# A two-layer transformer kernel on one core: the first normed input tiles made before the last two modulation blocks, their shift added in the rounding and in the remainder

## The chip, the core and the metric

The kernel runs on one core of one Trainium2 chip. A core has a matrix engine (TensorE, in the rows PE, its weight loads PEld), a vector engine (VectorE, DVE), an activation engine (ScalarE, ACT), a general engine (GpSimd, POOL) and a queue that issues transfers (SyncE, SP). Each works through its own list of instructions in order and waits on semaphores for the others. The metric is the time of one execution on the device, in microseconds (us), lower is better.

## What is computed

Two transformer blocks over 512 tokens of width 1024, in float32. The change touches the entry of the first block and its second normalisation:

```python
mod = jax.nn.silu(c) @ w_mod[layer] + b_mod[layer]
mod_c = jax.nn.silu(c_ctx) @ w_mod[layer] + b_mod[layer]
sh1, sc1, g1, sh2, sc2, g2 = jnp.split(mod[:, None, :], N_MOD, axis=-1)
...
h = modulate(rmsnorm(x, norm1_g[layer]), sh1, sc1)       # h * (1 + scale) + shift
hc = modulate(rmsnorm(ctx, norm1_g[layer]), sh1c, sc1c)
...
h2 = modulate(rmsnorm(x, norm2_g[layer]), sh2, sc2)      # and then the gated feed-forward part
```

`x` has 512 tokens, `ctx` 256. Everything behind `h` and `hc` (ten projections, neighbourhood attention, gated linear attention, the feed-forward part, the whole second block) follows from them.

## The kernel before

Activations lie transposed: a tile is 128 features by 512 tokens (a "page", one of 70), so `h` is eight tiles H0 to H7 and `hc` eight tiles HC0 to HC7 of 256 columns. Matrix products run in a split form: every operand is a rounded part (`hi`) and a remainder (`lo`), and each product is three matmuls, hi·hi, hi·lo and lo·hi (lines 1394, 1395, 1396). Weights come in 429 blocks of 128x1024 (`wst`). For a block ACT makes `whi` by a rounding copy (L1624) and POOL makes `wlo` by a subtraction (L2387); this pair is the step `w_split`. There are three raw buffers and four split ones, and the load of block b+3 waits for both halves of block b.

A planner written in Python (`planned`) lists all steps in one order, and each engine then emits its own part of each step in that order. So the place of a step in the list fixes who stands behind whom on each engine.

The entry of the first block runs like this. The modulation vectors come from `w_mod` in blocks of eight pages each: blocks 0 and 1 are the first and second half of the shift, blocks 2 and 3 those of the scale. The step `mod_rows(c)` is eight float32 matmuls with two rows of output (L1409) and a copy by ACT (L1648). The step `mod_columns` turns that row into columns on PE (L1418, 128x2) and adds the bias on DVE (L1893, into `modc`); for the scale DVE also makes A1 = (1 + scale)·gain (L1898). The statistics are squares on ACT (L1630), their sum over tiles on DVE (L1875), a product with a matrix of ones on PE (L1426), then `rstd_act` (L1639 logarithm, L1641 exponential, L1643 copy, with two table loads) and `rstd_dve` (L1881, L1884, L1886).

The step `h_in(k)` makes H(k) and HC(k). DVE multiplies by A1 and the reciprocal root (L1906, L1913) and adds the shift in place (L1909, L1916); ACT rounds (L1654, L1657); POOL subtracts (L2394, L2397). Tiles 0 to 3 use the first halves of shift and scale, tiles 4 to 7 the second. The first main product, called wide here, runs over k = 0 to 7 and for each k over two weight columns (`w_lr`, `wk_g`) and both H(k) and HC(k). Its four PSUM banks are those which the four `mod_columns` used before, so the fourth is free only when DVE has read the last of them (L1893).

Later, at 636 us, the second normalisation does the same with `h2_hi` (DVE L2119 scales, L2122 adds the shift; ACT L1764 rounds) and `h2_lo` (DVE L2128 subtracts), tile by tile between the steps of the first feed-forward product, and some position tables of the second block (L2165 to L2183 on DVE, L1787 to L1791 on ACT) are computed directly after it, ahead of the activation L1769 that frees banks for PE.

Of the kernel before, what the change touches and what calls it, by code (L numbers as in the profile page):

```python
# [10 lines left out]
ACT = mybir.ActivationFunctionType  # L11
# [306 lines left out]
def planned():  # L318
# [25 lines left out]
    for k in range(8, 16):  # L344
        mod_load(k)
    for k in range(24, 32):
        mod_load(k)
    step("load_fixed", "wal")
    step("load_fixed", "tabG")
    for b in range(1, NR):  # L350
        p.w_load(b)
# [5 lines left out]
    for k in range(8):  # L357
        sqc.add(("XC", k // 2), 256 * (k % 2), ("XC", k // 2))
# [16 lines left out]

    mod_rows(0)
    sqx.product("ones", sbk)
    mod_rows(2)
    mod_columns(0, 0)
    sqc.product("ones", sbk)  # L380
    rx = sqx.rstd(1024, "ones", sbk, True)
    mod_rows(1)
    mod_columns(0, 1)
    rc = sqc.rstd(1024, "ones", sbk, True)
    mod_rows(3)
    mod_columns(1, 0)
    for b in range(3):
        p.w_split(b)
    H, HC = [("H", k) for k in range(8)], [("HC", k) for k in range(8)]
    for k in range(8):  # L390
        if k == 4:
            mod_columns(1, 1)
# [5 lines left out]
        pages.give(("hct", k), ("HC", k, "hi"), ("HC", k, "lo"))  # L398
    pages.give(rx, ("hs", 7))
# [784 lines left out]
def program(nc, a, out, p):  # L1184
    with ExitStack() as ctx:
# [189 lines left out]
        def tensor(e):  # L1375
# [35 lines left out]

            def mod_columns(c, half_, part):
# [178 lines left out]
            def ret_values(l, h, i):  # L1591
# [9 lines left out]
                mm, mod_mm, mod_columns, square_sum, to_tokens, mod_sum, gla_gate, gla_state0, gla_states, gla_scores,  # L1601
# [6 lines left out]
        def scalar(e):  # L1608
# [42 lines left out]
            def h_in(k):  # L1651
                clear(("H", k, "hi"))
                w.wait_ge(*when("ht", k))
                e.activation(R(("H", k, "hi")), F(("ht", k)), ACT.Copy).then_inc(*acp.up(("H", k, "hi")))  # L1654
                clear(("HC", k))
                w.wait_ge(*when("hct", k))
                e.activation(R(("HC", k))[:, 0:256], F(("hct", k))[:, 0:256], ACT.Copy).then_inc(  # L1657
                    *acp.up(("HC", k, "hi")))
# [102 lines left out]
            def h2_hi(k):  # L1761
                clear(("H2", k, "hi"))
                w.wait_ge(*when("h2t", k))
                e.activation(R(("H2", k, "hi")), F(("h2t", k)), ACT.Copy).then_inc(*acp.up(("H2", k, "hi")))  # L1764
# [89 lines left out]
        def vector(e):  # L1854
# [46 lines left out]
            def h_in(k):  # L1901
                t, tc = F(("ht", k)), F(("hct", k))[:, 0:256]
# [3 lines left out]
                e.scalar_tensor_tensor(t, F(("X", k)), A1[:, k, 0:1], F(("r", "x")), ALU.mult, ALU.mult).then_inc(  # L1906
# [715 lines left out]
```

## Time and profile before

| | us |
|---|---|
| median of 3 runs | 3139.64 |
| lowest and highest of them | 3133.87, 3141.9 |
| the profiled execution | 3134.09 |
| its span, first to last instruction | 3132.3 |
| PE busy in the span | 2949.9 |
| DVE, ACT, POOL busy in the span | 1435.3, 1202.0, 1234.1 |

The span is that of the profiled execution; the rest of that execution's time, 1.8 us, lies around it. PE's busy time overlaps with its weight loads. The granted clock of TensorE is its mean over a stretch as a share of 2.4 GHz: 0.50 is 1.2 GHz, 1.00 is 2.4 GHz, and over the whole span it was 0.969.

### The profile page before, as it was taken

Reading aid. Unit: us, or ns where it says so; the run is one execution under the profiler, and the core shown is the slowest. Engines: PE = TensorE matmul, PEld = TensorE weight load, DVE = VectorE, ACT = ScalarE, POOL = GpSimd, SP = SyncE. Lnnn points to the kernel's source line nnn. Section 1 sums busy time; section 2 is a strip of 40 time slices with the busy share of each in tenths; the row PEclk is TensorE's granted clock in tenths of the full one; section 3 lists DMA queues with packets and bytes.
Section 4 is the critical chain, followed back from the end, with each engine's and each line's share of the span. In section 5 each row is a group of like instructions: output and inputs, shape, how many; then the busy total and the mean of one; then the engine's idle time right before and its main releaser. Section 6 shows DMA issues by size and latency. Waiting matters only on the chain.

```text
span 3132.3 us, 33658 instructions
## 1 busy us (share of the span) xinstructions
PE 2949.9 (94%) x13120; PEld 2296.9 (73%) x13120; DVE 1435.3 (46%) x1895; ACT 1202.0 (38%) x1737; POOL 1234.1 (39%) x571
## 2 busy tenths in 40 slices
PE   6998999989999898999998999989899999999997
PEld 2787777768888666678686888866666777778886
DVE  5667542451112778664524302257877354151123
ACT  3337653242223545342434322254533333342222
POOL 3213222334445344354343444434533444344442
PEclk8999999989999999999999999989999999999999
DMA  5233221322222210122131222221011222322221
GB/s 208 101 122 123 74 73 68 114 103 94 101 95 108 100 61 21 54 74 96 66 123 66 108 96 99 95 101 68 34 48 61 87 75 87 114 81 94 101 95 61
DMA packets 89342, 278.08 MB, mean 89 GB/s; under 512 B 10048, under 2 KB 10176, under 8 KB 89184
## 3 DMA queue, kind: packets, MB, share of 16 engines
q1 hardware_dynamic: 89184, 275.92, 24.3%
q8 instruction: 105, 1.72, 0.2%
q14 instruction: 53, 0.43, 0.0%
HBM read 268.54 MB, written 7.34 MB: 88 GB/s over the span
## 4 chain that ended last, share of the span: by engine, by line
PE 78%; DVE 15%; ACT 4%; issue 2%; DMA 1%; POOL 0%; SPq 0%; ACTq 0%; DVEq 0%; POOLq 0%
PE bank L1394 23%; PE bank L1396 22%; PE bank L1395 22%; PE bank L1597 2%; DVE pageF L2277 2%; PE bank L1439 1%; PE bank L1572 1%; PE bank L1560 1%; DVE pageF L2084 1%; PE bank L1549 1%; DVE pageF L2351 1%; DVE pageF L2355 1%; PE bank L1426 1%; PE bank L1409 1%; DVE pageR L2150 1%
## 5 line engine op out<-in xcount | busy, mean ns | idle before, releaser
L2387 POOL TENSOR_TENSOR wlo<-wraw,whi 128x1024 fp32r<-128x1024 f32 x429 | 1044.5, 2437 | 1624.8 <-ACT whi L1624 1612.8
L1394 PE MATMUL bank<-pageR,whi 128*128 128x512 f32 x3552 | 1451.7, 409 | 88.9 <-ACT pageR L1779 27.4
L1395 PE MATMUL bank<-pageR,whi 128*128 128x512 f32 x3552 | 1386.6, 390 | 0.0
L1396 PE MATMUL bank<-pageR,wlo 128*128 128x512 f32 x3552 | 1385.9, 390 | 0.0
L1394 PEld LDWEIGHTS bank<-pageR,whi 128*128 128x128 f32 x3552 | 677.3, 191 | 278.7 <-issue 126.4
L1395 PEld LDWEIGHTS bank<-pageR,whi 128*128 128x128 f32 x3552 | 678.5, 191 | 150.2 <-issue 23.6
L1396 PEld LDWEIGHTS bank<-pageR,wlo 128*128 128x128 f32 x3552 | 676.8, 191 | 141.3
L1624 ACT ACTIVATE whi<-wraw 128x1024 fp32r<-128x1024 f32 x429 | 450.5, 1052 | 403.1 <-PE bank L1396 400.0
L1663 ACT ACTIVATE pageR<-pageF 128x512 fp32r<-128x512 f32 x136 | 85.9, 632 | 427.1 <-DVE pageF L2144 207.9
L2277 DVE SCALAR_TENSOR_TENSOR pageF<-pageF,prm 128x497 f32<-128x497 f32 (+9 forms) x180 | 205.3, 1141 | 1.8
L1742 ACT ACTIVATE pageF<-bank,smal 128x512 f32<-128x512 f32 x96 | 66.0, 687 | 202.0 <-DVE smal L2058 201.7
L2139 DVE TENSOR_TENSOR pageF<-bank,pageF 128x512 f32<-128x512 f32 x44 | 30.4, 690 | 209.2 <-PE bank L1396 209.0
L1439 PEld LDWEIGHTS bank<-cst,pageF 128*128 128x128 f32 x564 | 69.4, 145 | 72.8 <-ACT pageF L1742 34.7
L1439 PE MATMUL bank<-cst,pageF 128*128 128x128 f32 x564 | 88.0, 283 | 36.7 <-ACT pageF L1742 22.9
L1875 DVE TENSOR_TENSOR pageF<-pageF 128x512 f32<-128x512 f32 (+1 forms) x60 | 43.6, 726 | 159.0 <-ACT pageF L1630 157.3
L2142 DVE TENSOR_TENSOR pageF<-pageF,bank 128x512 f32<-128x512 f32 x44 | 30.3, 688 | 182.4 <-PE bank L1396 177.4
L1693 ACT ACTIVATE pageF<-bank 128x512 f32<-128x512 f32 (+1 forms) x148 | 82.6, 575 | 80.0 <-PE bank L1439 79.4
L2426 POOL TENSOR_TENSOR pageF<-pageF 128x497 f32<-128x497 f32 (+14 forms) x60 | 79.2, 1320 | 79.8 <-ACT pageF L1826 78.6
L2406 POOL TENSOR_TENSOR pageR<-pageF,pageR 128x512 fp32r<-128x512 f32 x46 | 67.4, 1478 | 107.3 <-ACT pageR L1663 106.8
L2100 DVE SCALAR_TENSOR_TENSOR pageF<-pageF,bank 128x512 f32<-128x512 f32 x64 | 43.9, 685 | 126.8 <-PE bank L1396 126.6
L1923 DVE TENSOR_TENSOR pageR<-pageF,pageR 128x512 fp32r<-128x512 f32 x90 | 65.2, 724 | 64.8 <-ACT pageR L1663 64.8
L2133 DVE TENSOR_TENSOR pageF<-pageF,bank 128x512 f32<-128x512 f32 x22 | 15.1, 688 | 168.0 <-PE bank L1396 163.5
(200 smaller groups left out, 2386.1 us busy)
## 6 DMA issues: line engine op xcount, KB each, us to landing
wraw<-in_wst SPq DMA_DIRECT2D x429, 512.0 KB, 3.4
pageF<-in_wmod SPq DMA_DIRECT2D x96, 256.0 KB, 4.9
pageF<-in_xT SPq DMA_DIRECT2D x16, 256.0 KB, 5.3
pageF<-in_bias SPq DMA_DIRECT2D x16, 256.0 KB, 3.8
kept<-pageF SPq DMA_DIRECT2D x16, 256.0 KB, 4.7
pageF<-kept SPq DMA_DIRECT2D x16, 256.0 KB, 4.2
pageF<-tables SPq DMA_DIRECT2D x8, 256.0 KB, 4.7
out_x<-pageF SPq DMA_DIRECT2D x8, 256.0 KB, 2.0
```

What stands on the lines that cost most here:

```text
L1394: e.matmul(o, hi, xh, start=first, stop=False)
L1395: e.matmul(o, hi, xl, start=False, stop=False)
L1396: i = e.matmul(o, lo, xh, start=False, stop=last)
L1439: t = e.transpose(o[:, 128 * j:128 * j + 128], x[:, c:c + 128], ident)
L1624: e.activation(whi[:, b % NH, :, :], wraw[:, b % NR, :, :], ACT.Copy).then_inc(*whid.up(("whi", b)))
L1663: e.activation(R((*x, "hi")), F(src), ACT.Copy).then_inc(*acp.up((*x, "hi")))
L1693: e.activation(F(dst)[:, 0:n], bank(("tb", dst))[:, 0:n], ACT.Copy).then_inc(*acp.up(dst))
L1742: e.activation(F(("pr", kind, job)), bank(("sc", kind, job)), ACT.Exp, bias=nm, accum_out=sm).then_inc(*fun.up(("pr", kind, job)))
L2277: e.scalar_tensor_tensor(acc, x, c, acc, ALU.mult, ALU.add).then_inc(*vec.up(("tapd", l, m, n)))
L2387: e.tensor_tensor(wlo[:, b % NH, :, :], wraw[:, b % NR, :, :], bc(whi[:, b % NH, :, :]), ALU.subtract).then_inc(*wlod.up(("wlo", b)))
L2406: e.tensor_tensor(R((*x, "lo")), F(src), bc(R((*x, "hi"))), ALU.subtract).then_inc(*low.up((*x, "lo")))
L2426: e.tensor_tensor(acc, acc, F(("tap", l, n))[:, 0:hi - lo], ALU.add).then_inc(*low.up(("tapd", l, m, n)))
```

## The change

Five things are changed.

1. The order of transfers: the pages of `x` are loaded first, then shift and scale blocks 0 and 2, the context, weight block 0, then blocks 1 and 3 with weight blocks 1 and 2 behind them.
2. The order of steps: statistics of `x` go ahead of the squares of `ctx`; four `h_in` stand ahead of `mod_rows(1)` and `mod_rows(3)`; the three `w_split` are spread.
3. A step `warm_up`: six float32 matmuls of 128x512 on constants, in front of the first modulation product.
4. In `h_in` ACT adds the shift as a bias while it rounds, and the remainder is one DVE instruction (value plus shift, minus rounded). The two additions on DVE and the two subtractions on POOL are gone.
5. The same for `h2_hi` and `h2_lo`, where the remainder was on DVE already.

```diff
     for k in range(8):
-        mod_load(k)
-    for k in range(8):
         pages.take(("X", k))
         step("load_x", k)
-    for k in range(8):
-        mod_load(16 + k)
+    for c in (0, 2):
+        for k in range(8):
+            mod_load(8 * c + k)
...
+    sbk.take(("warm",))
+    step("warm_up")
+    sbk.give(("warm",), ("warm",))
     mod_rows(0)
     sqx.product("ones", sbk)
+    rx = sqx.rstd(1024, "ones", sbk, True)
+    for k in range(8):
+        sqc.add(("XC", k // 2), 256 * (k % 2), ("XC", k // 2))
     mod_rows(2)
     mod_columns(0, 0)
+    mod_columns(0, 1)
     sqc.product("ones", sbk)
...
+    p.w_split(0)
...
+    for k in range(4):
+        h_in(k)
+    mod_rows(1)
+    p.w_split(1)
+    mod_rows(3)
+    mod_columns(1, 0)
+    mod_columns(1, 1)
+    for k in range(4, 8):
+        h_in(k)
+    p.w_split(2)
...
+            def warm_up():
+                w.wait_ge(*when("cst"))
+                for i in range(6):
+                    t = e.matmul(bank(("warm",)), ident, cst[:, 0:4, :], start=True, stop=True)
+                t.then_inc(*dot.up(("warm",)))
...
-                w.wait_ge(*when("ht", k))
-                e.activation(R(("H", k, "hi")), F(("ht", k)), ACT.Copy).then_inc(*acp.up(("H", k, "hi")))
+                w.wait_ge(*when("hs", k))
+                e.activation(R(("H", k, "hi")), F(("ht", k)), ACT.Identity, bias=modc[:, k, 0:1]).then_inc(
+                    *acp.up(("H", k, "hi")))
...
-                after()
-                e.tensor_scalar(t, t, modc[:, k, 0:1], None, ALU.add).then_inc(*vec.up(("ht", k)))
...
+                w.wait_ge(*when("H", k, "hi"))
+                e.scalar_tensor_tensor(R(lo), F(("ht", k)), modc[:, k, 0:1], bc(R(("H", k, "hi"))), ALU.add,
+                                       ALU.subtract).then_inc(*vec.up(lo))
...
-                e.tensor_scalar(t, t, modr[:, 8 + k:9 + k], None, ALU.add).then_inc(*vec.up(("h2t", k)))
...
-                e.tensor_tensor(R(lo), F(("h2t", k)), bc(R(hi)), ALU.subtract).then_inc(*vec.up(lo))
+                e.scalar_tensor_tensor(R(lo), F(("h2t", k)), modr[:, 8 + k:9 + k], bc(R(hi)), ALU.add,
+                                       ALU.subtract).then_inc(*vec.up(lo))
```

PE, from its first instruction to the first product with H0, before. L1409 is a modulation product (x8 is one block), L1426 a sum of squares, L1418 the turning into columns.

```order
L1409 MATMUL bank<-pageF,csil 2x512 x8
L1426 MATMUL bank<-pageF,cst 128x512
L1409 MATMUL bank<-pageF,csil 2x512 x8
L1418 MATMUL bank<-cst,pageF 128x2 x4
L1426 MATMUL bank<-pageF,cst 128x256
L1409 MATMUL bank<-pageF,csil 2x512 x8
L1418 MATMUL bank<-cst,pageF 128x2 x4
L1409 MATMUL bank<-pageF,csil 2x512 x8
L1418 MATMUL bank<-cst,pageF 128x2 x8
L1394 MATMUL bank<-pageR,whi 128x512
```

The same stretch of the changed kernel, where lines 1415, 1438, 1430 and 1400 are those of the same four operations and 1421 is the new one.

```order
L1421 MATMUL bank<-cst 128x512 x6
L1415 MATMUL bank<-pageF,csil 2x512 x8
L1438 MATMUL bank<-pageF,cst 128x512
L1415 MATMUL bank<-pageF,csil 2x512 x8
L1430 MATMUL bank<-cst,pageF 128x2 x8
L1438 MATMUL bank<-pageF,cst 128x256
L1415 MATMUL bank<-pageF,csil 2x512 x16
L1430 MATMUL bank<-cst,pageF 128x2 x8
L1400 MATMUL bank<-pageR,whi 128x512
```

All four modulation products still stand ahead of the first main product; the second block's columns moved ahead of the products of the third and fourth.

ACT around the first rounded tiles, before: the last row copies (L1648), the weight roundings (L1624), then the tiles (L1654, L1657).

```order
L1643 ACTIVATE pageF<-bank,prm 128x256
L1648 ACTIVATE pageF<-bank 2x512
L1624 ACTIVATE whi<-wraw 128x1024 x3
L1654 ACTIVATE pageR<-pageF 128x512
L1657 ACTIVATE pageR<-pageF 128x256
```

And now, from the fourth tile (L1666, L1670) to the fifth, with the row copy at line 1660 and the weight rounding at 1636.

```order
L1666 ACTIVATE pageR<-pageF,modc 128x512
L1670 ACTIVATE pageR<-pageF,modc 128x256
L1660 ACTIVATE pageF<-bank 2x512
L1636 ACTIVATE whi<-wraw 128x1024
L1660 ACTIVATE pageF<-bank 2x512
L1666 ACTIVATE pageR<-pageF,modc 128x512
```

The last row copy, which PE's last turning and so the first main product wait for, now stands behind four tiles and two weight roundings.

DVE for one tile, before (first two rows H, then HC):

```order
L1906 SCALAR_TENSOR_TENSOR pageF<-pageF,A 128x512
L1909 TENSOR_SCALAR pageF<-pageF,modc 128x512
L1913 SCALAR_TENSOR_TENSOR pageF<-pageF,A 128x256
L1916 TENSOR_SCALAR pageF<-pageF,modc 128x256
L1906 SCALAR_TENSOR_TENSOR pageF<-pageF,A 128x512
```

And now:

```order
L1919 SCALAR_TENSOR_TENSOR pageF<-pageF,A 128x512
L1924 SCALAR_TENSOR_TENSOR pageF<-pageF,A 128x256
L1929 SCALAR_TENSOR_TENSOR pageR<-pageF,modc,pageR 128x512
L1934 SCALAR_TENSOR_TENSOR pageR<-pageF,modc,pageR 128x256
L1919 SCALAR_TENSOR_TENSOR pageF<-pageF,A 128x512
```

DVE still has four instructions a tile; two of them now wait for ACT's rounding, and POOL's two are gone.

## Rows read from the trace of the kernel before

**Rows 1.** The page, part 1: span, and each engine's busy time.

```profile
span 3132.3 us, 33658 instructions
PE 2949.9 (94%) x13120; PEld 2296.9 (73%) x13120; DVE 1435.3 (46%) x1895; ACT 1202.0 (38%) x1737; POOL 1234.1 (39%) x571
```

**Rows 2.** The chain that ended last, first 60 us: start us, us, what.

```profile
20.98 8.70 PE bank L1409 x16
...
30.66 6.96 PE bank L1409 x16
...
37.95 6.96 PE bank L1409 x16
...
47.06 2.33 DVE pageF L1916
49.39 2.76 DVE pageF L1906
```

**Rows 3.** The timeline, PE: start us, us, engine, line, what [idle before <-releaser].

```profile
55.88 0.77 PE L1394 MATMUL bank<-pageR,whi 128*128 128x512 f32 x1 [9.89 <-POOL pageR L2394]
...
64.50 0.58 PE L1394 MATMUL bank<-pageR,whi 128*128 128x256 f32 x1 [5.08 <-DVE modc L1893]
```

**Rows 4.** The first transfer of constants (timeline, then time to landing) and the squares of x.

```profile
1.65 0.42 SPq L1301 DMA_DIRECT2D cst<-in_cst  x1
...
cst<-in_cst SPq DMA_DIRECT2D x1, 320.0 KB, 3.1
...
12.65 4.68 ACT L1630 ACTIVATE pageF<-pageF 128x512 f32<-128x512 f32 x7 [0.34 <-DMA pageF<-in_xT]
```

**Rows 5.** The timeline, ACT and DVE, context squares, statistics and a row copy.

```profile
22.82 2.73 ACT L1630 ACTIVATE pageF<-pageF 128x256 f32<-128x256 f32 x8 [5.48 <-DMA pageF<-in_cT]
23.57 3.60 DVE L1875 TENSOR_TENSOR pageF<-pageF 128x256 f32<-128x256 f32 x7 [4.78 <-ACT pageF L1630]
...
30.33 1.28 ACT L1639 ACT_TABLE_LOAD   x1
...
34.16 0.67 ACT L1643 ACTIVATE pageF<-bank,prm 128x512 f32<-128x512 f32 x1
...
42.70 0.42 DVE L1886 SCALAR_TENSOR_TENSOR pageF<-pageF 128x256 f32<-128x256 f32 x1
...
44.94 0.59 ACT L1648 ACTIVATE pageF<-bank 2x512 f32<-2x512 f32 x1 [2.83 <-PE bank L1409]
```

**Rows 6.** Busy time by window: stretch, length, PE, PEld, DVE, ACT, POOL, PEclk, DMA share, GB/s.

```profile
64.40:68.80 4.40, 4.30 (x14) 3.72 (x15) 4.16 (x8) 1.47 (x3) 2.74 (x2) 0.50 0.02 6
68.80:75.00 6.20, 6.20 (x37) 5.41 (x37) 6.06 (x9) 2.11 (x4) 4.10 (x5) 1.00 0.00 0
...
667.40:672.90 5.50, 5.46 (x13) 4.38 (x14) 4.07 (x6) 2.69 (x4) 1.12 (x1) 0.50 0.00 0
```

**Rows 7.** The timeline, DVE and POOL, as the wide product ends.

```profile
79.77 7.03 POOL L2387 TENSOR_TENSOR wlo<-wraw,whi 128x1024 fp32r<-128x1024 f32 x3 [0.21 <-ACT whi L1624]
...
81.52 0.69 DVE L1931 TENSOR_TENSOR pageF<-bank,tabG 128x512 f32<-128x512 f32 x1 [3.29 <-PE bank L1396]
...
85.12 2.23 DVE L1938 TENSOR_TENSOR pageF<-pageF 128x512 f32<-128x512 f32 x1
```

**Rows 8.** Second normalisation, 635 to 668 us: single lines (durations ns min/median/max) and timeline.

```profile
L2119 DVE SCALAR_TENSOR_TENSOR pageF<-pageF,A x8: 742/746/2884, 635.8 to 649.8; 128x512 f32<-128x512 f32 x8
...
L2122 DVE TENSOR_SCALAR pageF<-pageF,modr x8: 485/486/488, 636.6 to 652.7; 128x512 f32<-128x512 f32 x8
...
638.15 0.68 DVE L2128 TENSOR_TENSOR pageR<-pageF,pageR 128x512 fp32r<-128x512 f32 x1
...
657.21 1.06 ACT L1624 ACTIVATE whi<-wraw 128x1024 fp32r<-128x1024 f32 x1 [2.38 <-PE bank L1396]
...
663.35 0.63 ACT L1787 ACTIVATE pageF<-pageF 128x512 f32<-128x512 f32 x1 [3.77 <-DVE pageF L2181]
...
666.70 0.60 ACT L1769 ACTIVATE pageF<-bank 128x512 f32<-128x512 f32 x1
...
667.44 0.77 PE L1394 MATMUL bank<-pageR,whi 128*128 128x512 f32 x1 [4.89 <-ACT pageF L1769]
```

More of the change, by code:

```diff
@@ L343, in planned @@
     p.w_load(0)
[L344 to L347, printed above, removed]
+    for c in (1, 3):
+        for k in range(8):
+            mod_load(8 * c + k)
+        p.w_load(1 + c // 2)
     step("load_fixed", "wal")
     step("load_fixed", "tabG")
-    for b in range(1, NR):
-        p.w_load(b)
     step("silu_c")
@@ L356, in planned @@
         sqx.add(("X", k), 0, ("X", k))
-    for k in range(8):
-        sqc.add(("XC", k // 2), 256 * (k % 2), ("XC", k // 2))
     def mod_rows(c):
@@ L1600, in tensor @@
             mine = {f.__name__: f for f in (
-                mm, mod_mm, mod_columns, square_sum, to_tokens, mod_sum, gla_gate, gla_state0, gla_states, gla_scores,
+                mm, mod_mm, warm_up, mod_columns, square_sum, to_tokens, mod_sum, gla_gate, gla_state0, gla_states, gla_scores,
                 gla_out, na_scores, na_values, mla_scores, mla_values, conv_mean, ret_scores, ret_values)}
@@ L1652, in h_in @@
                 clear(("H", k, "hi"))
-                w.wait_ge(*when("ht", k))
-                e.activation(R(("H", k, "hi")), F(("ht", k)), ACT.Copy).then_inc(*acp.up(("H", k, "hi")))
+                w.wait_ge(*when("hs", k))
+                e.activation(R(("H", k, "hi")), F(("ht", k)), ACT.Identity, bias=modc[:, k, 0:1]).then_inc(
+                    *acp.up(("H", k, "hi")))
                 clear(("HC", k))
-                w.wait_ge(*when("hct", k))
-                e.activation(R(("HC", k))[:, 0:256], F(("hct", k))[:, 0:256], ACT.Copy).then_inc(
-                    *acp.up(("HC", k, "hi")))
+                w.wait_ge(*when("hcs", k))
+                e.activation(R(("HC", k))[:, 0:256], F(("hct", k))[:, 0:256], ACT.Identity,
+                             bias=modc[:, k, 1:2]).then_inc(*acp.up(("HC", k, "hi")))
             def halves(x, src, made, lane):
@@ L1762, in h2_hi @@
                 clear(("H2", k, "hi"))
-                w.wait_ge(*when("h2t", k))
-                e.activation(R(("H2", k, "hi")), F(("h2t", k)), ACT.Copy).then_inc(*acp.up(("H2", k, "hi")))
+                w.wait_ge(*when("h2s", k))
+                e.activation(R(("H2", k, "hi")), F(("h2t", k)), ACT.Identity, bias=modr[:, 8 + k:9 + k]).then_inc(
+                    *acp.up(("H2", k, "hi")))
             def ffn_act(s, og, ou, r):
@@ L2120, in h2_hi @@
                     *vec.up(("h2s", k)))
-                after()
-                e.tensor_scalar(t, t, modr[:, 8 + k:9 + k], None, ALU.add).then_inc(*vec.up(("h2t", k)))
             def h2_lo(k):
@@ L2427, in tap @@
                     *low.up(("tapd", l, m, n)))
-            mine = {f.__name__: f for f in (w_split, h_in, halves, in_sum, tap)}
+            mine = {f.__name__: f for f in (w_split, halves, in_sum, tap)}
             for kind, *what in p.steps:
```

35 lines of the change are left out of this document (11 added, 24 removed).

## The prediction

> **What bounds the kernel now.** The page's first part comes first: PE is busy for 2949.9 of 3132.3 us [rows 1], so only about 180 us of the span are open to an edit that leaves PE's work alone, and this one does. I looked for them in the chain of waits and then in PE's timeline. In the first 60 us the chain runs through the four modulation products on PE and then through DVE [rows 2]: the fourth product ends at 37.95 + 6.96 = 44.9 us. From there on DVE instructions that should take 0.35 and 0.75 us take 2.33 and 2.76 us; they lie beside POOL's three weight subtractions. PE starts the wide product only at 55.88 us, released by POOL's remainder of H0, and after 3.3 us of it stands still again until 64.50 us, because DVE has not read the last modulation bank, which is queued behind four tiles [rows 3]. The clock is low there (0.50, 1.2 GHz) until 68.8 us [rows 6]. The second place is near 636 us: the chain is on DVE through the eight tiles and the tables behind them, and PE idles 4.89 us before 667.44 us [rows 8]. Elsewhere the change touches nothing.
>
> **The change, part by part.** I walk the changed order with durations of before, on the axis of the same profile.
>
> Warm-up and block 0. The constants are issued at 1.65 us and land 3.1 us later [rows 4], 4.8 us. A float32 matmul of 512 columns is two records; at the full clock 16 records take 6.96 us, 0.43 each, at the low one twice that [rows 2]. Twelve warm-up records thus cost 5.2 to 10.3 us; I take 8, half of them at each clock, so PE is free at 12.8 us. That costs nothing by itself: the pages of block 0 now come behind those of x, and the sixteenth page was there at about 16.7 us (the start of the last of the squares, 12.65 + 4.68 - 0.63) [rows 4]. Block 0 is then done at 12.8 + 6.9 = 19.7 us, the sum of squares at 20.6, block 2 at 27.5 (29.68 before, 20.98 + 8.70).
>
> Statistics. ACT does those of x first, two tables of 1.28 and three passes of about 0.65 us, [rows 5], 20.3 to 24.9 us. The context squares (2.73) follow to 27.6, the row copy (0.59) to 28.2. DVE does its three for x from 24.3 to 26.4 and then the seven context additions (3.60) [rows 5], to 30.0; these are later than before (27.2) and now set the pace. Then PE's sum 0.7, on ACT 0.47 + 1.28 + 0.42 + 0.46 (its table preloaded), DVE's three of 0.42: the context's reciprocal root is ready at about 34.6 us. It was ready at 42.70 + 0.42 = 43.1 us [rows 5], but the first tile had to wait for block 1 of the shift and DVE began it at 45.4. So the tiles begin 10.8 us earlier.
>
> Four tiles. Per tile DVE now has scale 0.69 and 0.42, a wait of about 0.28 for ACT's rounding (0.64 behind the first), remainder 0.69 and 0.45, 2.6 us with gaps. The remainder as one instruction with the shift doesn't exist before; between L2128's 0.68 and L2119's 0.75 [rows 8] the bounds are close, and I take 0.69. Rounding with a bias is bounded by the same operation from PSUM, 0.67 [rows 5], against 0.63 for the plain copy. The one weight subtraction in this stretch costs DVE one stall, 2.76 - 0.69 = 2.1 us [rows 2]. Four tiles: 34.6 + 2.1 + 10.4 = 47.1 us; ACT's last rounding there ends some 0.7 earlier, 46.4. Behind it on ACT stand the row copy, the weight rounding and the last row copy, 0.59 + 1.04 + 0.59 [rows 5, 8], 48.7 us, then 0.4 for the turning. PE's products of blocks 1 and 3 run from 30.6 to 44.6, or to 48.0 if the clock falls in the gap before them: hidden either way. **The wide product begins at 49.2 us**, and nothing in it waits: DVE frees the last bank at once, since it idles for just that column, and tiles 4 to 7 come every 2.6 us from 50 on, while PE needs the fifth at about 60.
>
> The wide product. Before, 3.3 us of it ran at the low clock before the stop, and 81.5 - 64.5 = 17.0 us behind it, 4.4 of these at the low clock [rows 3, 6, 7]. In one piece with 4.4 us at the low clock it lasts 20.3 - (3.3 / 2) = 18.7 us. It ends at 67.9, against 81.5: **13.6 us earlier**. Bounds: without the DVE stall and with a short low stretch 16; with two stalls and 3 us more on ACT's queue 10. Behind it DVE and PE alternate in the chain; all loads and weight steps hang on steps that moved too, so I let the whole shift pass. One stall of 1.5 us (L1938, 2.23 instead of 0.69, beside POOL's backlog [rows 7]) may go; POOL's fifth subtraction would end within 0.1 us of it, so I take 0 and keep 1.5 for the range.
>
> Of the shared path between DVE and POOL, the rows show that a DVE instruction with two SBUF tiles waits for a running POOL subtraction [rows 2] and that one fed from PSUM, L1931, does not [rows 7]. The Trainium skill, "SBUF — State Buffer", section "SBUF: two separate sides", says the same as an exclusive lock held for the whole instruction, and so speaks against putting 16 more remainders with two SBUF inputs on DVE. By it, each remainder could also hold off POOL's weight halves for its 0.69 us; the sum would be about 0.3 us worse.
>
> Second normalisation. Eight additions of 0.486 us leave DVE [rows 8]; the remainder grows by at most 0.07. The first remainder waits for one addition less of its own tile and one of the next, so PE starts 0.9 us earlier (638.1) and, being the slower from then on, ends this product at 661.6. DVE's tables start 3.4 earlier. But the rounding of the fourth weight block on ACT, which stands ahead of the table functions, waits for PE (L1624 at 657.21 [rows 8]), so it moves by 0.9 only: 656.3 + 1.06, table 1.28, first function at 658.6 (663.35 before). From that function to PE's restart it was 667.44 - 663.35 = 4.1 us [rows 8]: 662.7. **PE restarts 4.8 us earlier.** With one more DVE stall in the tables it is 3; if the gap, now 1.1 us, leaves the clock high, half of the 5.5 us at 0.50 [rows 6] come on top, 7.5 at most.
>
> Sum: 13.6 + 4.8 = 18.4 us. The profiled execution took 3134.1, so 3115.7; the median of before lies 5.5 higher, and against it the sum is 3139.6 - 18.4 = **3121.2, say 3121 us**.
>
> **Rivals.**
> The second place gives little: the tables' DVE instructions run into POOL's subtractions as before (L2119's longest was 2.884 us [rows 8]) and fill the gap. Then 13.6 alone, 3126. For it: two stalls of this kind are there now. Against: the additions are in the chain themselves.
>
> The head start is handed back: behind the wide product something pinned ends the gain, for instance modulation pages of the later blocks that arrive when they did. If only 3 us of the head survive: 3139.6 - 3 - 4.8 = 3132. For it: DVE holds much of the chain up to 200 us and the early transfers as a whole are no smaller. Against: the queue's order there is unchanged and each load waits for a page or a weight half that is earlier.
>
> Slower: TensorE's clock doesn't rise in the head. Then the warm-up and every modulation record costs 0.43 us more. Ahead of the wide product are 64 such records and the wide product's own start; at the low clock throughout they would add 64 x 0.43 = 27.5 us against a gain of 18.4, so 3149. It turns into a loss once 43 of the 64 records are slow. Against: in every busy stretch of before the clock rose within a few us (at 68.8 after work from 64.5 [rows 6]). The Trainium skill, "TensorE: Matmul & The Clock Gate", section "What's actually happening", has the low clock as the default after idling; by it the warm-up is lost again if PE then waits, as it will between 44.6 and 49.2, and I have priced the wide product's start as low for that reason.
>
> **How the numbers follow.** Main case 0.62 (3114 to 3127), only the head 0.17 (3126), handed back 0.13 (3132), low clock 0.04 (3149), and 0.04 for no difference at all. The range takes the largest gain, 16 + 1.5 + 7.5 = 25, with the runs' own spread (the lowest of before lies 5.8 under its median) down to 3109, and the smallest, 10 + 3 = 13, plus 4 for the median's own uncertainty, up to 3131. A difference of 0.3%, 9.4 us, is about the least that can be told from none here: the line is at 3130.2. Faster: 0.62 + 0.17 and a third of the handed-back case, 0.83. Slower by as much: 0.04. Within: 0.13.
>
> **What would show it.** In the changed profile: block 2's product ends near 27.5; the first DVE scale at 34.6, the first L1400 at 49.2 with no second stop; the low clock ends by 54; the rope multiplication (L1931 before) starts at 67.9; each later landmark up to 600 us stands 13 to 14 us earlier. At the second place the idle time before PE's restart is 1 us, not 4.9. I am wrong if the first L1400 is past 53, if the shift at 300 us is under 10, or if DVE's remainders take over 1 us on average.

## The result and the profile after

The changed kernel takes 3116.2 us in the median of 4 runs (3112.3 to 3118.1); the kernel before, beside it, 3136.8 (3133.2 to 3141.9). The ratio is 0.9932, 95% interval 0.9912 to 0.9951. The forecast was 3121, in a range of 3109 to 3131.

The page's first part answers to [rows 1]:

```profile
span 3115.6 us, 33638 instructions
PE 2952.5 (95%) x13132; PEld 2298.8 (74%) x13132; DVE 1419.1 (46%) x1887; ACT 1203.0 (39%) x1737; POOL 1217.3 (39%) x555
```

The span is 16.7 us shorter, PE's work the same but for 12 warm-up records; DVE lost 16 us and POOL 17. How much of either was in the way is a matter of places. PE in the head, to set beside [rows 2, 3] (timeline: start us, us, engine, line, what, count, [idle before <-releaser]):

```profile
6.37 8.45 PE L1421 MATMUL bank<-cst 128*128 128x512 f32 x12 [6.37 <-DMA cst<-in_cst]
14.76 7.03 PE L1415 MATMUL bank<-pageF,csil 128*2 128x512 f32 x16
21.72 1.12 PE L1438 MATMUL bank<-pageF,cst 128*128 128x512 f32 x2
22.77 7.03 PE L1415 MATMUL bank<-pageF,csil 128*2 128x512 f32 x16
...
32.78 15.59 PE L1415 MATMUL bank<-pageF,csil 128*2 128x512 f32 x32
48.70 0.41 PE L1430 MATMUL bank<-cst,pageF 2*128 2x2 f32 x4 [0.33 <-ACT pageF L1660]
50.13 0.40 PE L1430 MATMUL bank<-cst,pageF 2*128 2x2 f32 x4 [1.02 <-ACT pageF L1660]
50.46 0.50 PE L1400 MATMUL bank<-pageR,whi 128*128 128x512 f32 x1
```

PE's 9.89 us of waiting ahead of the first main product and the stop of 5.08 us inside it are gone; blocks 1 and 3 now run beside the tiles. DVE, ACT and POOL in that stretch:

```profile
36.38 0.74 DVE L1919 SCALAR_TENSOR_TENSOR pageF<-pageF,A 128x512 f32<-128x512 f32 x1
37.05 2.57 DVE L1924 SCALAR_TENSOR_TENSOR pageF<-pageF,A 128x256 f32<-128x256 f32 x1
...
42.25 0.75 DVE L1929 SCALAR_TENSOR_TENSOR pageR<-pageF,modc,pageR 128x512 fp32r<-128x512 f32 x1 [0.39 <-ACT pageR L1666]
...
45.03 0.75 DVE L1929 SCALAR_TENSOR_TENSOR pageR<-pageF,modc,pageR 128x512 fp32r<-128x512 f32 x1 [0.40 <-ACT pageR L1666]
...
67.27 0.69 DVE L1950 TENSOR_TENSOR pageF<-bank,tabG 128x512 f32<-128x512 f32 x1 [3.97 <-PE bank L1402]
67.99 2.84 DVE L1954 TENSOR_TENSOR pageF<-bank,tabG 32x512 f32<-32x512 f32 x4
70.87 2.72 DVE L1957 TENSOR_TENSOR pageF<-pageF 128x512 f32<-128x512 f32 x1
...
44.28 0.72 ACT L1666 ACTIVATE pageR<-pageF,modc 128x512 fp32r<-128x512 f32 x1 [1.66 <-DVE pageF L1919]
...
48.56 1.04 ACT L1636 ACTIVATE whi<-wraw 128x1024 fp32r<-128x1024 f32 x1
49.50 0.57 ACT L1660 ACTIVATE pageF<-bank 2x512 f32<-2x512 f32 x1
...
36.55 2.79 POOL L2405 TENSOR_TENSOR wlo<-wraw,whi 128x1024 fp32r<-128x1024 f32 x1 [36.11 <-ACT whi L1636]
49.74 2.38 POOL L2405 TENSOR_TENSOR wlo<-wraw,whi 128x1024 fp32r<-128x1024 f32 x1 [10.40 <-ACT whi L1636]
63.48 9.56 POOL L2405 TENSOR_TENSOR wlo<-wraw,whi 128x1024 fp32r<-128x1024 f32 x4 [11.36 <-ACT whi L1636]
```

One remainder starts 2.78 us after the other (45.03 - 42.25), which is the time of a tile. The rope multiplication (L1950, DVE's first step on the wide product's result) stands at 67.27, [rows 7] had it at 81.52: 14.3 us gained.

Second normalisation, PE's two starts, the fourth weight block's rounding and first table function on ACT, and DVE's table steps:

```profile
628.68 0.77 PE L1400 MATMUL bank<-pageR,whi 128*128 128x512 f32 x1 [7.51 <-DVE pageR L2145]
...
654.24 0.47 PE L1400 MATMUL bank<-pageR,whi 128*128 128x512 f32 x1 [1.14 <-ACT pageF L1783]
...
647.76 1.06 ACT L1636 ACTIVATE whi<-wraw 128x1024 fp32r<-128x1024 f32 x1 [4.38 <-PE bank L1402]
...
650.14 0.63 ACT L1801 ACTIVATE pageF<-pageF 128x512 f32<-128x512 f32 x1
...
643.86 2.51 DVE L2194 TENSOR_SCALAR pageF<-pageF 128x512 f32<-128x512 f32 x1
...
648.58 0.43 DVE L2199 TENSOR_SCALAR pageF<-pageF 128x512 f32<-128x512 f32 x1
```

The restart moved from 667.44 [rows 8] to 654.24, 13.2 us, 3.8 of them won here (the shift just ahead was 9.4), and the low clock that followed it in [rows 6] is absent, which gives 2.5 more.

POOL lost time here, too. Its first weight subtraction in this stretch lasts 5.70 us, and 2.86 in the kernel before:

```profile
632.39 5.70 POOL L2405 TENSOR_TENSOR wlo<-wraw,whi 128x1024 fp32r<-128x1024 f32 x1 [14.33 <-ACT whi L1636]
...
635.08 0.74 DVE L2138 SCALAR_TENSOR_TENSOR pageF<-pageF,A 128x512 f32<-128x512 f32 x1
```

and before:

```profile
643.58 2.86 POOL L2387 TENSOR_TENSOR wlo<-wraw,whi 128x1024 fp32r<-128x1024 f32 x1 [15.98 <-ACT whi L1624]
```

In the changed kernel DVE ran scalings and remainders without a gap until 635.82 us, and 2.3 us later POOL was done. The timeline shows no wait of PE's between 628.68 and 654.24 us, so PE lost nothing by it.

To see where the shift grows and shrinks, I paired PE's matmuls of two traces one by one, counted from the end (fillers left out), and took the difference of their starts. Times are on the axis of before. "Changed" is the profiled run above; "again" and "beside" are two more of the same kernel; the experiments of the other rows follow below. The last column is the whole shift.

| us | 70 | 100 | 140 | 300 | 320 | 600 | 660 | 690 | end |
|---|---|---|---|---|---|---|---|---|---|
| changed | -14.3 | -15.9 | -13.6 | -14.9 | -10.4 | -9.5 | -9.4 | -15.8 | -16.7 |
| again | -13.6 | -15.2 | -15.3 | -12.6 | -11.9 | -11.4 | -11.6 | -17.9 | -19.1 |
| beside | -12.8 | -14.4 | -14.7 | -13.7 | -13.7 | -13.6 | -14.1 | -17.2 | -18.4 |
| head only | -15.4 | -17.0 | -15.0 | -16.4 | -16.4 | -16.4 | -16.5 | -16.4 | -17.9 |
| second place only | -0.3 | -0.3 | 0.2 | 5.5 | 5.9 | 6.2 | 6.0 | 2.8 | 1.7 |
| order only | -9.1 | -10.8 | -10.5 | -10.6 | -10.6 | -10.6 | -10.6 | -10.5 | -11.9 |
| instructions only | -0.7 | -2.3 | 1.8 | 0.3 | 0.3 | 0.3 | -0.1 | -3.3 | -4.6 |
| no warm-up | -12.9 | -14.5 | -10.1 | -11.4 | -6.8 | -5.9 | -5.8 | -12.1 | -12.9 |
| rows first | -15.5 | -17.1 | -12.4 | -13.9 | -13.9 | -13.8 | -14.3 | -17.4 | -18.6 |
| fillers | -15.0 | -16.6 | -14.8 | -16.9 | -16.8 | -16.8 | -19.1 | -20.2 | -21.4 |
| tables late | -16.6 | -18.2 | -18.3 | -18.3 | -18.3 | -18.3 | -18.6 | -26.0 | -26.4 |
| tables late, fillers | -15.8 | -17.4 | -16.8 | -14.3 | -13.6 | -13.1 | -15.5 | -22.8 | -23.1 |

The 1.6 us that every row but "second place only" gains from 70 to 100 us come between 84 and 90 us. The kernel before is at the low clock there (85.9 to 89.3 us), as is "second place only", and the others are not at that work.

### The profile page after: what moved, and what is told of

Same layout as the page of the kernel before. It is cut to its first block, busy times and chain, and to the rows that moved or that the text cites. A ratio compares the mean times of both kernels' runs of the same rounds, so it can differ in the third digit from the quotient of the medians.

```text
span 3115.6 us, 33638 instructions
## 1 busy us (share of the span) xinstructions
PE 2952.5 (95%) x13132; PEld 2298.8 (74%) x13132; DVE 1419.1 (46%) x1887; ACT 1203.0 (39%) x1737; POOL 1217.3 (39%) x555
## 4 chain that ended last, share of the span: by engine, by line
PE 78%; DVE 15%; ACT 4%; issue 2%; DMA 1%; POOL 1%; SPq 0%; DVEq 0%; ACTq 0%; POOLq 0%
PE bank L1400 23%; PE bank L1402 22%; PE bank L1401 22%; PE bank L1609 2%; DVE pageF L2295 2%; PE bank L1451 1%; PE bank L1584 1%; PE bank L1572 1%; PE bank L1561 1%; DVE pageF L2103 1%; DVE pageF L2373 1%; DVE pageF L2369 1%; DMA pageF<-in_wmod 1%; DVE pageR L2168 1%; PE bank L1600 1%
## 5 line engine op out<-in xcount | busy, mean ns | idle before, releaser
L1676 ACT ACTIVATE pageR<-pageF 128x512 fp32r<-128x512 f32 x136 | 85.9, 632 | 425.0 <-DVE pageF L2162 208.1
L2160 DVE TENSOR_TENSOR pageF<-pageF,bank 128x512 f32<-128x512 f32 x44 | 30.2, 687 | 182.4 <-PE bank L1402 177.4
L1889 DVE TENSOR_TENSOR pageF<-pageF 128x512 f32<-128x512 f32 (+1 forms) x60 | 43.0, 717 | 149.6 <-ACT pageF L1642 148.0
L1895 DVE TENSOR_TENSOR pageF<-pageF 128x512 f32<-128x512 f32 (+1 forms) x41 | 26.9, 656 | 141.5 <-ACT pageF L1653 141.5
```

What stands on the lines that cost most here:

```text
L1676: e.activation(R((*x, "hi")), F(src), ACT.Copy).then_inc(*acp.up((*x, "hi")))
```

## The experiments

My theory was that of the prediction: the head and the second place are two separate gains, the head's being that the tiles no longer wait for blocks 1 and 3 and that POOL's remainders and DVE's additions are out of the way. The rivals were that one of the two gives nothing, that it is all order (or all instructions), and that the clock decides.

### Each place alone

Head only: the second normalisation keeps its old instructions.

```diff
-                e.scalar_tensor_tensor(R(lo), F(("h2t", k)), modr[:, 8 + k:9 + k], bc(R(hi)), ALU.add,
-                                       ALU.subtract).then_inc(*vec.up(lo))
+                e.tensor_tensor(R(lo), F(("h2t", k)), bc(R(hi)), ALU.subtract).then_inc(*vec.up(lo))
...
+                e.tensor_scalar(t, t, modr[:, 8 + k:9 + k], None, ALU.add).then_inc(*vec.up(("h2t", k)))
```

> The changed kernel with its second normalisation put back (DVE adds the shift, ACT copies, plain subtraction). Theory A (the two places add up, as the shift between the two traces says: 14.3 us at the end of the wide product, 4 us more at PE's restart near 667 us and some 2 us of clock behind it): 4 to 6 us slower than the changed kernel, so 14 to 17 us faster than before, ratio 0.995. Its PE idle time before the restart is again 4 to 5 us. Rival B (the tables' DVE work would have been hidden anyway): within 1.5 us of the changed kernel.

Measured 3118.4 us (3116.1 to 3124.0), ratio 0.9954, interval 0.9941 to 0.9966: 16.9 us under the median of before beside it, as expected, but only 2 us over the changed kernel's median, where 4 to 6 were expected. PE's wait before its restart is 4.94 us, and its shift does not move between 600 and 690 us. Second place only: the kernel before with the opposite of this diff and nothing else.

> The kernel before with only the second normalisation changed. Theory A: 4 to 6 us faster than before, ratio 0.9985; nothing differs ahead of 636 us, PE's idle time before the restart falls from 4.9 to about 1 us. Rival B: no difference.

Measured 3133.2 us (3127.0 to 3138.1), ratio 0.9992, interval 0.9983 to 1.0002: for itself not to be told from nothing. Its trace shows a gain all the same, 3.4 us between 600 and 690 us in the table. That is under the 4 to 6 expected, and PE's wait before its restart fell to 2.72 us and not to 1. The 5.5 us it lost before 300 us lie where no instruction differs from the kernel before, nearly all of them in one low-clock stretch of 10.2 us at 218.7 us. The kernel before has no such stretch there, and in this trace no wait of PE's stands right ahead of it.

So both places give. In the traces of the table the whole head is worth 12.8 to 16.6 us at 70 us, and the second place, with the tables where they were, 3.4 to 6.5.

### Order and instructions, apart

Order only: the changed order of loads and steps with the warm-up, but the old instructions at both places (shift added by DVE, remainder of H on POOL).

```diff
-                w.wait_ge(*when("hs", k))
-                e.activation(R(("H", k, "hi")), F(("ht", k)), ACT.Identity, bias=modc[:, k, 0:1]).then_inc(
-                    *acp.up(("H", k, "hi")))
+                w.wait_ge(*when("ht", k))
+                e.activation(R(("H", k, "hi")), F(("ht", k)), ACT.Copy).then_inc(*acp.up(("H", k, "hi")))
```

> The new order of transfers and steps and the warm-up, but all normed tiles by the old instructions (shift by a DVE addition, remainders of the first tiles on POOL). Theory A (the order is most of the gain, the instructions set the pace of a tile): a tile takes DVE 3.4 us, as tiles 4 to 7 did before, against 2.6, so four tiles cost 3.2 us more and the wide product starts at about 53.7 us instead of 50.5 and ends at 71; with the old second normalisation the whole is 10 to 11 us faster than before. Rival C (the fused instructions are most of the gain, since DVE and POOL block each other): under 5 us faster than before.

Measured 3126.1 us (3122.2 to 3130.8), ratio 0.9975, interval 0.9966 to 0.9985. Its DVE and PE:

```profile
46.87 1.37 DVE L1921 TENSOR_SCALAR pageF<-pageF,modc 128x512 f32<-128x512 f32 x1
...
51.44 0.58 PE L1430 MATMUL bank<-cst,pageF 2*128 2x2 f32 x4 [4.44 <-ACT pageF L1660]
...
53.37 0.80 PE L1400 MATMUL bank<-pageR,whi 128*128 128x512 f32 x1
```

In the second and the fourth tile DVE's additions, beside POOL's remainders, take 1.3 to 1.4 us; one at 55.68 us, with POOL at rest, took 0.49. The first four tiles last from 35.50 to 50.45 us, 15.0, where the changed kernel has 12.8 (36.38 to 49.14). PE waits 4.44 us, starts the main product 2.9 us later than the changed kernel, and is at the low clock for 6.8 us from 51.4 on. So the start was 53.4 us for the 53.7 expected.

Instructions only: the kernel before with the new instructions at both places, old order, no warm-up (the edit is the reverse of the one above, in the kernel before).

> The new instructions in both places, but the old order of transfers and steps and no warm-up. Theory A: the first main matmul waits for POOL's first weight half (49.2 us), PE stops again until DVE has done four tiles with three stalls, 45.4 + 4 x 2.6 + 3 x 2.1 = 62 us (64.5 before), so some 2.5 us at the head and 5 at the second place: 6 to 9 us faster than before. Rival C: over 12 us faster than before.

Measured 3131.0 us (3127.6 to 3135.6), ratio 0.9992, interval 0.9983 to 1.0001: 4 us, less than I expected, and within the interval nothing. PE and DVE:

```profile
52.25 0.77 PE L1394 MATMUL bank<-pageR,whi 128*128 128x512 f32 x1 [5.99 <-DVE pageR L1923]
...
63.05 0.58 PE L1394 MATMUL bank<-pageR,whi 128*128 128x256 f32 x1 [6.04 <-DVE modc L1901]
...
49.29 2.81 DVE L1923 SCALAR_TENSOR_TENSOR pageR<-pageF,modc,pageR 128x512 fp32r<-128x512 f32 x1 [2.52 <-ACT pageR L1660]
```

The main product starts 3.6 us earlier than in [rows 3], not at the 49.2 us expected, and then stands still for 6.0 us instead of 5.1: the last bank still waits behind four tiles. At 70 us order alone has 9.1 us, instructions alone 0.7, both together 14.3 (13.6 and 12.8 in the other two traces). The sum of the parts is 9.8, so 3.0 to 4.5 us are in neither alone.

It is not that PE waits for something else in the old order: it waits for these tiles there too. But the first tile gives back what is saved. DVE's first remainder now needs ACT's rounding, which stands behind three weight roundings, and DVE idles 2.52 us for it. Then two weight subtractions hold DVE up (2.81 us for the remainder shown, 2.46 for the next). The four tiles take 17.2 us instead of 18.9. And the low clock lasts until 69 us in both kernels, so that of 1.45 us of shift at 68 us 0.7 are left at 70. The new order spreads the three weight roundings, and a tile then costs 2.8 us.

The order of transfers and the order of steps were only ever changed together; what each gives alone is open.

### The warm-up

```diff
-    sbk.take(("warm",))
-    step("warm_up")
-    sbk.give(("warm",), ("warm",))
```

> The changed kernel without its six warm-up matmuls. Theory A (the warm-up is neutral: without it the first modulation product starts when its first page has landed, near 12 us, at the low clock, and ends near 21.5 us as it does now, at 21.8): within 2 us of the changed kernel. Rival D (the warm-up carries the head: later modulation products stay at the low clock without it): 5 us or more slower than the changed kernel, with the wide product starting at 55 us or later.

Measured 3115.6 us (3115.3 to 3121.2), ratio 0.9933, interval 0.9919 to 0.9946, the same as with it. Its shift at 70 us is -12.9, within the -12.8 to -14.3 of the three traces with it, and its main product starts at 50.27 us; so much for the rival's 55. Its first product starts earlier and takes longer, and ends at 21.64 us, with the warm-up at 21.79:

```profile
13.00 8.64 PE L1412 MATMUL bank<-pageF,csil 128*2 128x512 f32 x16 [13.00 <-DMA pageF<-in_wmod]
```

### The last row copy ahead of the weight rounding

In the changed kernel the copy that PE's last turning waits for stands behind a weight rounding of 1.04 us. This moves it ahead.

```diff
     mod_rows(1)
-    p.w_split(1)
     mod_rows(3)
     mod_columns(1, 0)
     mod_columns(1, 1)
+    p.w_split(1)
```

> The changed kernel with the second weight block's rounding behind the last two row copies and the turning instead of between them. If the wide product waits for ACT's queue, as the chain of the changed kernel says (the last row copy starts at 49.50 us, right behind a rounding of 1.04 us, while PE's product was done at 48.4): it starts 0.9 us earlier and the kernel is 0.5 to 1.5 us faster than the changed one, too little to be told in its time but plain in its trace. If something else ends that wait: the start stays at 50.4 to 50.5 us.

Measured 3113.3 us (3108.9 to 3115.5), ratio 0.9923, interval 0.9911 to 0.9936. The main product starts at 49.24, not 50.46, and 70 us is reached 1.2 us earlier than in the changed kernel. The median is 2.9 us lower, but the intervals overlap.

### The clock at the second place

Eight filler matmuls stand in PE's wait for the second normalisation; nobody reads their product, and nothing is left out.

```diff
         r = sq.rstd(1024, "ones", sbk, warm=True)
+        sbk.take(("warm2",))
+        step("warm_up", "warm2", 8)
+        sbk.give(("warm2",), ("warm2",))
```

> The changed kernel with eight idle float32 matmuls on constants put into PE's wait for the second normalisation (7.5 us idle at 621 to 628.7 us). Its output is not touched. If the low clock behind that wait is due to the idling: the granted clock stays at 1.00 there, PE's product after it runs at full speed from the start, and PE gains 2.5 us, of which up to 1.5 may be handed back where PE then waits for the tables; kernel 1 to 2.5 us faster. If the clock falls whatever PE does there: no gain, low clock until 634 us as now.

Measured 3118.0 us (3112.7 to 3122.3), ratio 0.994, interval 0.9926 to 0.9954: no gain. PE's two starts there:

```profile
621.44 0.47 PE L1403 MATMUL bank<-pageR,whi 128*128 128x512 f32 x1 [0.64 <-DVE pageR L2149]
...
647.05 0.77 PE L1403 MATMUL bank<-pageR,whi 128*128 128x512 f32 x1 [3.57 <-ACT pageF L1787]
```

The clock did stay high, and the shift at 650 us was 2.3 us larger than ahead of the place. But PE then waits 3.57 us for the gate's eviction (L1787, ACT emptying the bank that PE needs) behind the tables' ACT passes, and works at the low clock again. In this trace a clock bought ahead of a join with a slower engine was mostly idle time at the join.

### The same kernel again, twice

> The changed kernel once more, for a second trace. Between 300 and 350 us the changed kernel lost 4.5 us of its lead in the first trace, where PE stood still for 4.7 us in both kernels and the low clock behind it lasted 13.7 us instead of 3.4. If that is a matter of the single execution: another length of the low stretch here, and another lead at 350 us. If it belongs to the change: 13.7 us again.

3115.0 us, its only run. Low-clock stretches have other lengths in it than in the first profile. The clearest case is around 290 us, where PE waits 4.6 to 4.9 us in every trace. Windows of the changed kernel (stretch, length, busy time of PE, PEld, DVE, ACT, POOL, then PEclk, DMA share, GB/s):

```profile
290.00:295.00 5.00, 5.00 (x15) 4.08 (x16) 4.96 (x6) 2.57 (x6) 2.57 (x1) 0.50 0.26 100
295.00:300.00 5.00, 5.00 (x17) 3.94 (x16) 2.06 (x5) 0.32 (x1) 0.19 (x1) 0.50 0.73 241
300.00:305.00 5.00, 5.00 (x24) 4.33 (x23) 1.97 (x4) 0.46 (x2) 0.00 (x0) 0.73 0.21 77
```

and of the run beside the last two kernels below:

```profile
290.00:295.00 5.00, 3.80 (x15) 3.15 (x15) 4.90 (x8) 3.82 (x9) 1.32 (x1) 0.66 0.48 172
295.00:300.00 5.00, 5.00 (x30) 4.21 (x30) 4.42 (x8) 0.78 (x2) 1.43 (x1) 1.00 0.47 155
```

13.7 us of low clock (1.2 GHz) in the first, 3.4 us in the second, with the same instructions. It is this that took the first profile from -14.9 to -10.4 us at 300 to 320 us; it is no cost of the change.

### Tables behind the first gates

The experiment that follows from the two above: if PE's restart waits for the tables' passes on ACT, plan the tables one slot later (and keep the rows first).

```diff
     def side_tables():
+        yield from pause(1)
         pages.take(("posi",))
```

> The changed kernel with two moves: the second weight block's rounding stands behind the last two row copies (as in the run of that one move), and the position tables' plan starts one slot later, so that the first sine table's load and three ACT passes (1.28 + 0.63 + 0.64 + 0.72 us) stand behind the first two gates of the feed-forward's wide group and not ahead of them. Theory: in the traces PE stood 1.1 us (changed kernel) or 2.7 us (the run with the rows first) before its restart for the gate's eviction that waits for those passes, and in the second of these a low clock of 3.4 us followed. With the tables behind, PE's wait there is at most 0.8 us and no low clock follows: 2 us + 1.7 us better than the run with the rows first at 690 us (shift against the kernel before about -21 there, -17.4 in that run), median near 3110 against its 3113.3. Rival: the tables' passes only push the later gates back, the wait turns up again within 20 us, and the time stays at 3113.

> As the run before it, plus eight filler matmuls in PE's wait for the second normalisation, whose product nobody reads (the work the kernel needs is all there). In the earlier run with fillers PE kept the full clock through its restart and was 2.3 us ahead at 650 us, and gave that back because it then waited for the tables' ACT passes and fell to the low clock for 6.8 us. Theory: with the tables out of the way the 2.3 us stay: shift at 690 us about -23, median near 3108. Rival: the time at 690 us is set by ACT and DVE, not by PE's clock, and both runs agree within 1 us.

> The changed kernel itself, unaltered, beside the two above on the same chip: 3116 within its spread of 3112 to 3118. Its low clock behind PE's wait near 290 us should again have another length than 13.7 us if that is a matter of the single execution (3.4, 6.8 and 13.7 us have been seen with the same wait), and its shift at 320 us should then be nearer to the -14.9 it had at 300 us.

On one chip: tables late 3108.5 us (3106.2 to 3112.7), ratio 0.9903, interval 0.9886 to 0.9919; with fillers too 3110.4 (3105.8 to 3113.3), 0.9904, 0.9890 to 0.9919; the changed kernel 3114.9 (3113.1 to 3115.7), 0.9919, 0.9905 to 0.9934; the kernel before 3140.3. The ranges of tables late and of the changed kernel do not touch, though the intervals of the ratios still overlap a little. ACT and the clock at the restart, tables late:

```profile
643.24 0.60 ACT L1784 ACTIVATE pageF<-bank 128x512 f32<-128x512 f32 x1
...
654.13 0.63 ACT L1802 ACTIVATE pageF<-pageF 128x512 f32<-128x512 f32 x1 [5.97 <-DVE pageF L2200]
...
644.00:649.00 5.00, 5.00 (x22) 4.13 (x23) 3.57 (x6) 2.71 (x4) 0.67 (x1) 1.00 0.19 78
```

The timeline shows no wait of PE's left there, and the clock stays high. Between 600 and 690 us the shift grows by 7.7 us, with rows first it was 3.6: this place gives 4.1 us more, about as expected (3.7). Against the traces in which PE's wait there was 1.14 us and no low clock followed (below) it is only 1.2 to 1.5 us more. The other 4.5 us between the two at 690 us are there at 600 us already, and arise from 105 to 125 us, where rows first had a PE wait of 3.46 us and a low clock that this execution had not. That part I can't credit to the edit.

The fillers do nothing for the median here either, but the trace shows that their theory held once the tables were out of the way. PE's restart after the statistics, tables late first, then with fillers:

```profile
619.96 0.76 PE L1401 MATMUL bank<-pageR,whi 128*128 128x512 f32 x1 [7.50 <-DVE pageR L2146]
...
625.08 0.47 PE L1404 MATMUL bank<-pageR,whi 128*128 128x512 f32 x1 [0.64 <-DVE pageR L2150]
```

The kernel with fillers comes to this place 5.1 us behind the other, is 3.2 behind from 624 us on, and still 3.2 at 720 us and 3.3 at the end: 1.9 us gained and kept, as against 2.3 gained and handed back with the tables in the way. What hides it in the span was lost before 320 us, where no instruction differs: 3.3 of the 5.1 us between 195 and 220 us, where this trace has two low-clock stretches of 3.4 us that the other has not. With four runs of each kernel and a spread of 6 to 8 us the medians can't show 2 us.

The third run settles what the second place is worth. DVE there and the windows at its restart, the run of the changed kernel beside:

```profile
639.33 2.50 DVE L2192 TENSOR_SCALAR pageF<-pageF 128x512 f32<-128x512 f32 x1
...
644.50 2.53 DVE L2199 TENSOR_SCALAR pageF<-pageF 128x512 f32<-128x512 f32 x1
...
651.17 0.47 PE L1400 MATMUL bank<-pageR,whi 128*128 128x512 f32 x1 [2.71 <-ACT pageF L1783]
...
651.00:656.00 5.00, 4.83 (x14) 3.87 (x15) 3.51 (x6) 2.72 (x5) 0.49 (x1) 0.66 0.00 0
```

Two of DVE's table steps are stretched from 0.43 to 2.5 us by POOL's weight subtractions, not one; PE waits 2.71 us instead of 1.14, and 3.4 us of low clock follow. Of the seven traces with the new second place, no fillers and the tables where they were, three (changed, again, no warm-up) have one stretched step, 1.14 us and a high clock, and gain 6.2 to 6.5 us between 600 and 690; four (second place only, instructions only, rows first, beside) have two, 2.70 to 2.72 us and a low clock, and gain 3.4 to 3.6.

## Why the prediction was right

The median came out 4.8 us under the forecast. Of these, 2.9 are the base: I had counted from a median of before of 3139.6, and beside the changed kernel it was 3136.8. Against that the gain is 20.6 us, and in the three profiled executions of the changed kernel, against the one of before, 16.7, 19.1 and 18.4; the sum was 18.4. That it fits so well is in part luck: single low-clock stretches move an execution by several us, and the second place came out at 4.8 only as a mean (below). Point by point:

**The head start** was 13.6 us, bounds 10 to 16. Measured 14.3, and 13.6 and 12.8 in the other two. The steps on the way were less exact than the sum. The constants landed at 6.37 and not at 4.8 us, and the warm-up took 8.45 and not 8.0, so block 2 ended at 29.8, not at 27.5. I had called the warm-up's place free because the pages of block 0 would arrive last (16.7 us); without it, though, the product began at 13.0. It is still free, because the product is slower without it.

**The tiles** began at 36.4, forecast 34.6, for the same reason, and took 2.78 us each, forecast 2.6: rounding with a bias is 0.72 us, where I had bounded it by 0.67, the remainder 0.75, where I had taken 0.69 between 0.68 and 0.75, and DVE's wait for ACT 0.40 where I had 0.28. The one stall of 2.1 us came as priced (L1924, 2.57 instead of 0.48). The four tiles ended at 49.1, forecast 47.1.

**The wide product** began at 50.46, forecast 49.2, and had no second stop. That I was 1.3 us late there and 0.6 early at its end is the clock: I had taken 4.4 us of it at the low one.

```profile
33.00:36.40 3.40, 3.40 (x5) 0.51 (x4) 1.21 (x4) 3.37 (x5) 0.00 (x0) 0.50 1.05 387
36.40:48.30 11.90, 11.90 (x28) 2.21 (x26) 10.43 (x16) 4.72 (x9) 2.79 (x1) 1.00 0.58 218
50.40:55.40 5.00, 5.00 (x30) 4.36 (x29) 4.33 (x7) 1.12 (x2) 1.72 (x1) 1.00 0.30 105
```

It was low from 33.0 to 36.4 us instead, inside the products of blocks 1 and 3, which ended at 48.4. In "again" and "beside" 3.4 us of the wide product were at the low clock, against 4.4 forecast: rope at 67.9 and 68.7. So the term was there in two executions of three. What decides it is open. PE stood 0.33 us before the first turning in the profiled run and 1.0 to 1.1 us in those two, but without the warm-up it stood 0.34 us and the low clock came, and with the rows first 1.06 us and it did not.

**Nothing saved at rope** held: the stall behind it is 2.72 us (L1957), where [rows 7] had 2.23.

**The whole shift passes on** held within 2.2 us, 70 against 600 us, in seven of the ten traces of the table that have a head start (head only: -15.4 and -16.4). In tables late with fillers 2.7 us were lost, and in the other two, changed and no warm-up, 4.8 and 7.0, and I would have called it wrong by the first profile alone, at 320 us. The rival of a head start handed back, with 3 us left, is out: the least that any of them has at 600 us is 5.9. What moves the shift between 100 and 600 us, by as much as 8.6 us (no warm-up), is in part the length of single low-clock stretches, which differs between traces of one kernel. Another part are waits of PE for DVE: at 89.08 us PE waits 4.02 us in the first profile, 2.35 and 2.36 in again and beside, and 1.90 in the kernel before (its 102.85).

**The second place** was 4.8 us, bounds 3 to 7.5, and this term was mis-sized though the total was not. No trace has 4.8 between 600 and 690 us: it is 6.2 to 6.5 or 3.4 to 3.6, by one DVE stall more or less and the clock behind it. PE's restart itself moved by 3.8 us beyond the shift ahead of it in the three traces with one stall and by 2.2 in the four with two, where the prediction had 4.8 and 3. The clock made up for it: it stayed high, or was low for 3.4 us instead of 6.8. The prediction knew both effects, but only as the ends of its range; that their mean is near 4.8 is luck.

The step that failed is the start. PE did start 0.8 us earlier (0.9 forecast), but had nothing of it a few us later (shift -10.3 at 638.98, -9.6 at 643.11), because it was still at the low clock, and the clock rose 8.5 us earlier than before, less than PE's own shift of 9.5. So the fourth weight rounding moved by no more than the head, 9.45. The first table function came at 650.1 us, where 658.6 less that head start would be 649.2. The rival "second place gives little" (13.6 alone, 3126) is out by the 3.4 us at least in every such trace, against none in head only. The medians alone don't decide it: head only, 3118, and the changed kernel are 2 us apart, which their intervals don't tell apart.

**The low-clock rival** (3149) needed 43 of the head's 64 modulation records at the low clock. Only the few that ran between 33.0 and 36.4 us were.

**POOL held off by the remainders.** The Trainium skill, "SBUF — State Buffer", section "SBUF: two separate sides", has DVE and POOL hold each other off for a whole instruction, and the prediction gave about 0.3 us for it. That was far too little for the delay, though not for the time of the kernel. In the second normalisation one weight subtraction takes 5.68 to 5.70 us in all ten traces with the new instructions there. Without them (before, head only, order only) no weight subtraction takes over 3.2 us. It ends 2.3 us after DVE's unbroken row of scalings and remainders, so it was held off for the rest of the row, 3.3 us, and not for one instruction, as the Trainium skill has it. PE didn't wait for it. In the head the first subtraction, which began while the scaling L1919 ran, took 2.79 us and the next 2.38, and POOL idled for 10 us behind it.

## What to carry to other kernels

When a step's operands arrive in blocks, let it start on the first blocks and put the rest of their making beside it; a shorter instruction sequence for the step paid only with that (0.7 us alone, 3.7 to 5.2 on top of the order), because in the old order its first tile waited for a rounding queued behind three others. Look behind every join of engines for what is queued ahead of the instruction that frees the waiting one, on its own in-order engine: there one planned slot for an unrelated side task was worth 4 us in the trace against the less lucky of two cases, and 1.2 to 1.5 against the better. Keeping PE's clock high was handed back as long as that task stood in the way, and worth 1.9 us in the trace when it didn't. And don't judge a part by one profiled execution where a stall or a clock step can fall either way; two or three traces of one kernel differed here by 3 us at 320 us.

## What the runs showed of the hardware

The low clock behind one and the same wait of 4.6 to 4.9 us, before the same matmuls, lasted 3.4 us (the kernel before, beside, and six others), 6.8 us (again, second place only, tables late with fillers) or 13.7 us (changed, no warm-up).

A POOL subtraction can be held off by a whole row of DVE instructions, not only by the one that runs when it starts: 5.70 us instead of 2.39, with DVE at work without a gap until 635.82 us (L2138 and L2145 in turn, each with two tiles in SBUF). It isn't always so. In the head POOL's subtraction at 36.55 us was done in 2.79, and the DVE instruction behind L1919 waited; in the kernel before the one at 643.58 us was done in 2.86, and the scaling at 644.10 us waited, 2.88. What decides who goes first is open.

DVE waits for a running POOL subtraction with one SBUF input too, not only with two: L2199, a scalar operation on one page, took 2.53 us with POOL busy from 644.35 for 2.40, and 0.43 in the first profile. A DVE operation with an input from PSUM was not held up: L1950 and L1954 took 0.69 and 0.71 us each with POOL busy from 63.48 for 9.56 us, and L1957, the next, with SBUF alone, 2.72. The Trainium skill, "SBUF — State Buffer", section "SBUF: two separate sides", has DVE and POOL lock each other out where DVE has two SBUF inputs or works in a mode that uses two ports. That agrees with L1957; whether L2199 ran in such a mode, no run here shows.

An ACT pass over 128x512 that adds a per-partition bias took 0.72 us from SBUF, a plain copy of the same size 0.63 (order only, L1666). Adding the shift in the rounding is cheap, 0.09 us for a DVE instruction of 0.49 [rows 8], but not free.
